# The second attention of a two-block layer: 64 units as one sequence, and the first branch's transposes beside projection panels

## What is computed

```python
def token_mixer(h, w_in, w_a2, b_a, b_f, g_gla, w_pa, w_pb, w_out):
    z = h @ w_in
    q_a, k_a, v_a, a_low, r_a, q_b, k_b, v_b, f_b, gate_a, gate_b = jnp.split(z, cuts, axis=-1)
    o_a = gla_chunked(heads(q_a * GLA_HK ** -0.5), heads(k_a), heads(v_a), heads(log_a))  # 4 heads
    o_a = rmsnorm_2(o_a, g_gla).reshape(B, T, GLA_DV) * jax.nn.silu(r_a)
    logf = jax.nn.log_sigmoid(f_b + b_f)
    o_b = fox_attention(heads(q_b), heads(k_b), heads(v_b), logf)       # 16 heads of 64
    merged = jax.nn.sigmoid(gate_a) * (o_a @ w_pa) + jax.nn.sigmoid(gate_b) * (o_b @ w_pb)
    return merged @ w_out
# fox_attention: logit[t,s] = q_t.k_s/8 + F_t - F_s with F = cumsum(logf), causal softmax, times v
```

## Time and profile before

| | |
|---|---|
| median of 3 runs | 2513.05 us (2510.02 to 2513.66) |
| the profiled execution | 2510.3 us, its span 2508.5 us |
| PE busy | 2365.5 us, 94% of the span |
| DVE, ACT, POOL busy | 948.3, 929.6, 1037.7 us |
| mean granted clock of PE | 0.961 of full speed |
| the stretch of the change | from 1703 to 1994 us of the span |

### The profile page before, as it was taken

How to read it: one execution, slowest core, us unless ns; L and a number is a source line. 1 busy time by engine, 2 the same in 40 slices (tenths; PEclk the granted TensorE clock), 3 DMA queues, 4 the chain that set the end, 5 groups by cost and what they waited for, 6 DMA issues and landing times.

```text
span 2508.5 us, 34111 instructions
## 1 busy us (share of the span) xinstructions
PE 2365.5 (94%) x10556; PEld 1922.4 (77%) x10556; DVE 948.3 (38%) x1601; ACT 929.6 (37%) x1628; POOL 1037.7 (41%) x796
## 2 busy tenths in 40 slices
PE   7999987899999998999997999998999997999997
PEld 6888866778888887888876777776666786888886
DVE  5699967435514214100114144444333343110012
ACT  4333374234322323333333533344333353443331
POOL 4455354444444443444453433332112254444443
PEclk9999998999999999999997999998899997999998
DMA  4334342437737432333331233333111331333331
GB/s 147 97 97 114 118 130 76 147 101 279 274 102 251 134 91 73 96 97 96 97 96 51 80 110 96 96 99 123 34 33 38 113 93 50 93 96 101 96 96 59
DMA packets 130557, 267.90 MB, mean 107 GB/s; under 512 B 14352, under 2 KB 14480, under 8 KB 129712
## 3 DMA queue, kind: packets, MB, share of 16 engines
q1 hardware_dynamic: 119520, 236.51, 31.4%
q10 hardware_dynamic: 10960, 30.38, 3.2%
HBM read 252.12 MB, written 14.68 MB: 106 GB/s over the span
## 4 chain that ended last, share of the span: by engine, by line
PE 82%; issue 7%; DVE 6%; POOL 3%; ACT 2%; DMA 0%; DVEq 0%; ACTq 0%; POOLq 0%
PE bank L851 24%; PE bank L853 23%; PE bank L852 23%; POOL wlo L374 2%; PE bank L1156 2%; PE bank L1188 1%; PE bank L1051 1%; PE bank L1053 1%; PE bank L1052 1%; PE bank L1102 1%; PE bank L1158 1%; PE bank L1170 1%; PE bank L1120 1%; DVE tmp L1507 1%; PE bank L961 1%
## 5 line engine op out<-in xcount | busy, mean ns | idle before, releaser
L374 POOL TENSOR_TENSOR wlo<-raw,whi 128x512 fp32r<-128x512 f32 x750 | 983.5, 1318 | 1365.9 <-ACT whi L446 1364.7
L851 PE MATMUL bank<-a_hi,whi 128*128 128x512 f32 x1992 | 797.0, 400 | 18.4 <-DVE a_lo L1261 7.1
L853 PE MATMUL bank<-a_lo,whi 128*128 128x512 f32 x1992 | 784.2, 394 | 0.0
L852 PE MATMUL bank<-a_hi,wlo 128*128 128x512 f32 x1992 | 784.0, 394 | 0.0
L446 ACT ACTIVATE whi<-raw 128x512 fp32r<-128x512 f32 x750 | 466.4, 627 | 776.6 <-PE bank L853 657.5
L851 PEld LDWEIGHTS bank<-a_hi,whi 128*128 128x128 f32 x1992 | 378.4, 190 | 113.6 <-issue 18.4
L853 PEld LDWEIGHTS bank<-a_lo,whi 128*128 128x128 f32 x1992 | 378.6, 190 | 80.8
L852 PEld LDWEIGHTS bank<-a_hi,wlo 128*128 128x128 f32 x1992 | 379.5, 191 | 74.5
L851 PE MATMUL bank<-b_hi,whi 128*128 128x512 f32 x788 | 316.5, 402 | 27.1 <-DVE G L1521 11.4
L852 PE MATMUL bank<-b_hi,wlo 128*128 128x512 f32 x788 | 312.1, 396 | 0.0
L853 PE MATMUL bank<-b_lo,whi 128*128 128x512 f32 x788 | 311.9, 396 | 0.0
(11 more groups left out here) (234 smaller groups left out, 1887.4 us busy)
## 6 DMA issues: line engine op xcount, KB each, us to landing
raw<-d_stream SPq DMA_DIRECT2D x750, 256.0 KB, 2.6
G<-d_ada SPq DMA_DIRECT2D x72, 512.0 KB, 4.6
spill_rv<-tmp ACTq DMA_DIRECT2D x32, 256.0 KB, 2.1
G<-spill_rv ACTq DMA_DIRECT2D x6, 1024.0 KB, 10.3
G<-d_x ACTq DMA_DIRECT2D x4, 512.0 KB, 5.4
spill_ga<-G ACTq DMA_DIRECT2D x8, 256.0 KB, 3.5
spill_gb<-G ACTq DMA_DIRECT2D x8, 256.0 KB, 3.5
G<-spill_ga ACTq DMA_DIRECT2D x1, 2048.0 KB, 8.1
```

Source lines behind the costliest of these rows:

```text
L374: pool.tensor_tensor(wlo[:, s % SRING, :], raw[:, s % RING, :], whi[:, s % SRING, :].bitcast(F32), ALU.subtract).then_inc(lo_done, 1)
L851: pe.matmul(out_ps, w_hi, hi[:, k, :], start=first and q == 0, stop=False)
L852: pe.matmul(out_ps, w_lo, hi[:, k, :], start=False, stop=False)
L853: mm = pe.matmul(out_ps, w_hi, lo[:, k, :], start=False, stop=last and q == len(ks) - 1)
```

## The change

Three things are done.

1. The four turns become one sequence of 64 units on PE, ACT and DVE, without loops: `scores(u + 2)` stands in every unit up to 61, and the first two scores stand once, ahead of everything. `QF`'s slots are chosen by the head's pair, and `keep_qk` follows in fixed units.
2. Tiles 2 and 3 of `qkb` are no longer done ahead. Two half panels follow the first two scores, and six stand between the eight groups of transposes of the first branch.
3. These transposes go to banks 4 and 5, since banks 6 and 7 now hold the scores of units 0 and 1. ACT takes their exponentials after the last product (`r_prod`) and ahead of its eight roundings, and DVE their maxima between the products and the scalings.

The work itself is the same: 64 half panels of `qkb` (16 ahead of unit 0's transposes, then one in each of 48 units), the same transposes, scores and products.

```diff
@@ -754,57 +755,61 @@
...
-def keep_qk(i, j):
+def keep_qk(j):
+    wait_used(act, "qkb", 0, 2 * j + 1)
     act.activation(QF[:, j % 4, :], bank_of("qkb", j)[:, :], ACT.Copy,
                    scale=FOX_HD ** -0.5 if j % 2 == 0 else 1.0).then_inc(evac_of("qkb", j), 1)
...
-for j in range(4):
+def fox_exp(u):
+    n = (u % 4 + 1) * P
+    act.wait_ge(fox_m, u + 1)
...
+for j in range(2):
     tick("qkb", 0, 2 * j)
-    wait_used(act, "qkb", 0, 2 * j + 1)
-    keep_qk(0, j)
-    if j == 1:
-        act.wait_ge(ld_r, 32)
-        for t in range(4):
-            act.activation(R2[:, t, :], R2[:, t, :], ACT.Silu).then_inc(r_silu, 1)
+    keep_qk(j)
+act.wait_ge(ld_r, 32)
+for t in range(4):
+    act.activation(R2[:, t, :], R2[:, t, :], ACT.Silu).then_inc(r_silu, 1)
+tick("qkb", 0, 4, 1)
+act.wait_ge(r_prod, 2 * GLA_HEADS)
+fox_exp(0)
+fox_exp(1)
 for m in range(KD):
     act.wait_ge(b_val, m + 1)
     act.activation(b_hi[:, m, :], tmp[:, m % 2, :], ACT.Copy).then_inc(b_hi_w, 1)
-def fox_turn(i, next_qk):
-    for u in range(17):
-        if u < 16:
-            n = (u % 4 + 1) * P
...
-        if next_qk and u < 16 and u % 2 == 0:
-            tick("qkb", i, 8 + u // 2, 1)
-        if not next_qk and u < 16 and u % 4 < 3:
-            tick("pa", 0, 3 * (u // 4) + u % 4, 1)
-        if next_qk and u in (9, 11):
-            keep_qk(i, 4 + u // 10)
-    if next_qk:
-        for j in (6, 7):
-            wait_used(act, "qkb", i, 2 * j + 1)
-            keep_qk(i, j)
-with act.Fori(0, FOX_HEADS // 4 - 1) as i:
-    fox_turn(i, True)
-fox_turn(FOX_HEADS // 4 - 1, False)
...
+    if m % 2 and m < 7:
+        tick("qkb", 0, 5 + m // 2, 1)
+    if m == 5:
+        keep_qk(2)
+for u in range(UNITS + 1):
+    if 2 <= u < UNITS:
+        fox_exp(u)
+    if u:
...
+        act.activation(PT[:, w % 2, 0:n], bank[4 + w % 2][:, 0:n], ACT.Copy).then_inc(fox_pt, 1)
+    if u == 1:
+        keep_qk(3)
+    if u < UNITS - 16:
+        if u % 2 == 0:
+            tick("qkb", 0, 8 + u // 2, 1)
+    elif u < UNITS and u % 4 < 3:
+        v = u - (UNITS - 16)
+        tick("pa", 0, 3 * (v // 4) + v % 4, 1)
+    if u > 8 and u % 8 in (1, 3) and u // 8 < 7:
+        keep_qk(2 * (u // 8 + 1) + u % 8 // 2)
...
@@ -1121,80 +1126,81 @@
...
-for j in range(4):
+def scores(u):
+    h, t = u // 4, u % 4
+    n = (t + 1) * P
+    r = slice(FOX_HD * (h % 2), FOX_HD * (h % 2 + 1))
+    at = h // 2 % 2 * 2
...
+def qk_half(q):
+    j, k = q // 4, 2 * (q % 4)
+    if k == 0:
+        bank_free("qkb", 0, j)
+    panel("qkb", 0, q // 2, (k, k + 1), bank_of("qkb", j)[:, :], OPA, k == 0, k == 6, q0=k % 4,
+          done=q % 2 == 1)
...
+for j in range(2):
     tile8("qkb", 0, j, OPA, opa, fill, False)
+pe.wait_ge(gla_exp, GLA_HEADS * len(GLA_EXP) + 1)
+scores(0)
+scores(1)
+qk_half(8)
+qk_half(9)
 pe.wait_ge(r_prod, 2 * GLA_HEADS)
 for m in range(KD):
     if m >= 2:
         pe.wait_ge(b_val, m - 1)
     for t in range(4):
-        mm = pe.transpose(bank[6 + m % 2][:, t * P:(t + 1) * P],
+        mm = pe.transpose(bank[4 + m % 2][:, t * P:(t + 1) * P],
                           ONH[:, m // 2, t, m % 2 * P:(m % 2 + 1) * P], ident)
     mm.then_inc(oa_t, 1)
+    if m < 6:
+        qk_half(10 + m)
...
-    scores(0)
-    scores(1)
-    for u in range(16):
-        h, t = u // 4, u % 4
-        pe.wait_ge(fox_p, i * 16 + (u + 3))
-        pe.wait_ge(fox_out, i * 16 + (u + 1))
-        for j in range(t + 1):
-            c = slice(j * P, (j + 1) * P)
-            mm = pe.transpose(bank[4 + u % 2][:, c], PR[:, u % 2, c], ident)
-        mm.then_inc(fox_t, 1)
-        if u < 14:
-            scores(u + 2)
-        if next_qk:
...
-with pe.Fori(0, FOX_HEADS // 4 - 1) as i:
-    fox_turn(i, True)
-fox_turn(FOX_HEADS // 4 - 1, False)
-pe.wait_ge(fox_out, 64 + 2)
+for u in range(UNITS):
+    h, t = u // 4, u % 4
+    pe.wait_ge(fox_p, u + 3)
+    if u < 2:
+        pe.wait_ge(b_val, KD - 1 + u)
+    pe.wait_ge(fox_out, u + 1)
+    for j in range(t + 1):
...
+    if u < UNITS - 2:
+        scores(u + 2)
+    if u < UNITS - 16:
+        qk_half(16 + u)
+    elif u % 4 < 3:
+        if u == UNITS - 16:
+            pe.wait_ge(opb, FILL_B["oa"] + KD)
+        pa_panel(3 * ((u - (UNITS - 16)) // 4) + u % 4)
+    pe.wait_ge(fox_pt, u + 3)
...
+dve.wait_ge(ld_f, 16)
+forget_sums(0)
...
+maximum(0)
+maximum(1)
...
-with dve.Fori(0, FOX_HEADS // 4 - 1) as i:
-    own.begin(i, 16 * 2)
-    fox_turn(i, False)
-    own.end(FOX_HEADS // 4 - 1)
-fox_turn(FOX_HEADS // 4 - 1, True)
+beside = [UNITS - 16 + u for u in (1, 4, 6, 9, 12, 14)]
+for u in range(UNITS):
+    h, t = u // 4, u % 4
+    if u < UNITS - 2:
+        maximum(u + 2)
+    if t == 0 and h < FOX_HEADS - 1:
+        forget_sums(h + 1)
```

More of the change, by code:

```diff
@@ L40 @@
 TAU = 16.0
+UNITS = 4 * FOX_HEADS
 RING, SRING, AHEAD = 8, 4, 3
@@ L1122, in _, with pa_panel @@
                         mm.then_inc(gla_mm, 1)
-            for j in range(4):
-                tile8("qkb", 0, j, OPA, opa, fill, False)
+            def scores(u):
[3 more added lines that the diff above has]
+                at = h // 2 % 2 * 2
+                s_ps = bank[6 + u % 2][:, 0:n]
+                pe.wait_ge(fox_p, u + 1)
+                if t == 0:
+                    pe.wait_ge(fox_nf, h + 1)
+                    wait_evac(pe, "qkb", 0, h // 2 * 2)
+                    wait_evac(pe, "qkb", 0, h // 2 * 2 + 1)
+                pe.matmul(s_ps, QF[r, at, t * P:(t + 1) * P], QF[r, at + 1, 0:n], start=True, stop=False)
+                pe.matmul(s_ps, ONES_R[32:64, :], NFH[32:64, h % 2, 0:n], start=False, stop=True)\
+                  .then_inc(fox_s, 1)
+            def qk_half(q):
[4 more added lines that the diff above has]
+                      done=q % 2 == 1)
+            def pa_panel(p):
+                if p % 2 == 0:
+                    bank_free("pa", 0, p // 2)
+                half = p % 2
+                panel("pa", 0, p, range(4 * half, 4 * half + 4), bank_of("pa", p // 2)[:, :], OPB, half == 0, half == 1)
+            for j in range(2):
+                tile8("qkb", 0, j, OPA, opa, fill, False)
+            pe.wait_ge(gla_exp, GLA_HEADS * len(GLA_EXP) + 1)
[3 more added lines that the diff above has]
+            qk_half(9)
             pe.wait_ge(r_prod, 2 * GLA_HEADS)
@@ L1193, in _ @@
-            with pe.Fori(0, FOX_HEADS // 4 - 1) as i:
-                fox_turn(i, True)
-            fox_turn(FOX_HEADS // 4 - 1, False)
-            pe.wait_ge(fox_out, 64 + 2)
+            for u in range(UNITS):
[5 more added lines that the diff above has]
+                for j in range(t + 1):
+                    c = slice(j * P, (j + 1) * P)
+                    mm = pe.transpose(bank[4 + u % 2][:, c], PR[:, u % 2, c], ident)
+                mm.then_inc(fox_t, 1)
+                if u < UNITS - 2:
[7 more added lines that the diff above has]
+                pe.wait_ge(fox_pt, u + 3)
+                for j in range(t + 1):
+                    mm = pe.matmul(bank[4 + u % 2][:, 0:FOX_HD], PT[:, u % 2, j * P:(j + 1) * P],
+                                   VB[:, j, h * FOX_HD:(h + 1) * FOX_HD], start=j == 0, stop=j == t)
+                mm.then_inc(fox_o, 1)
@@ L1198, in _ @@
+            pe.wait_ge(fox_out, UNITS + 2)
             for m in range(KD):
@@ L1790, in _ @@
-            with dve.Fori(0, FOX_HEADS // 4 - 1) as i:
-                own.begin(i, 16 * 2)
-                fox_turn(i, False)
-                own.end(FOX_HEADS // 4 - 1)
-            fox_turn(FOX_HEADS // 4 - 1, True)
+            beside = [UNITS - 16 + u for u in (1, 4, 6, 9, 12, 14)]
[5 more added lines that the diff above has]
+                    forget_sums(h + 1)
+                dve.wait_ge(fox_o, u + 3)
+                own.next(dve.reciprocal(small[:, 1, u % 2:u % 2 + 1], small[:, 5, t:t + 1]))
+                dve.tensor_scalar(OB[:, t, h * FOX_HD:(h + 1) * FOX_HD], bank[4 + u % 2][:, 0:FOX_HD],
+                                  small[:, 1, u % 2:u % 2 + 1], None, ALU.mult).then_inc(fox_out, 1)
+                if u in beside:
+                    keep_pa(beside.index(u))
```

107 lines of the change are left out of this document (25 added, 82 removed).

## The result

The changed kernel takes 2481.59 us, the median of 4 runs (2479.68 to 2487.65), beside 2513.36 for 4 runs of the kernel before (2510.02 to 2514.64). The ratio is 0.9884, with a 95% interval of 0.987 to 0.9898. The forecast was 2491 us with a range of 2486 to 2501, so the direction was right and the gain came out as 31.8 us instead of 21.6. Measured again beside other runs of the kernel before, the gain was 26.7 and 29.2 us (experiments 1 and 9), so some 3 to 5 us of the first figure are chance, and the rest of the miss is not.

A forecast was written before the change was run, and what follows sets the result against it. PE was taken to bound the kernel, gaining only where idle or at half clock. Seams 16.8, head 0 3.1 and unit 0's start 1.7 sum to 21.6 us, taking the median 2513.05 to 2491 us, range 2486 to 2501.

The forecast's parts named there:

- What bounds the kernel: Whole kernel: PE bounds it, so time is gained only where PE stands idle or runs at half clock.
- Behind unit 52, nothing: After unit 52: nothing changes; falls of the clock there may come or stay away, 1.7 us each.
- The seams, 16.8 us: Between the four turns: idle time and half clock at three seams, 7.53 + 6.35 + 2.92, all go, 16.8 us.
- Written-out code instead of a loop costs nothing: Attention turns: replacing the loop by written-out code has no cost, judged by turn 3, already written out.
- Pairs: Rival: scores of each new pair of heads wait for `keep_qk` at seven places, 2498 us and up; chance 0.04.
- Head 0, 3.1 us: Units 0 to 4: 3.37 us above a normal head, laid to half clock, mostly goes; gain 3.1 us.
- When unit 0 starts, 1.7 us: Start of the attention: unit 0's transposes begin at 1739.7 instead of 1741.44, a gain of 1.7 us.
- a pause of 3.8 us: Ahead of the first branch's transposes: PE newly waits for the products, from 1720.1 to 1723.9, 3.8 us.
- groups of 1.97 us: First branch's transposes: four transposes and a half panel take 1.97 us per group, six times, 11.8 us.
- The clock loss of 2.5 us: After the new pause: half clock delays unit 0 by 2.5 us, with ends of 0 and 8.5 us.
- Both together: Start of unit 0 and head 0: gains of 1.7 and 3.1 us, 4.8 us in all.
- The clock stays low at the start: Rival: half clock persists into head 0, costing 6.3 or 4.7 us, 2497 us in all; chance 0.22.

The follow-up runs named there:

- experiment 1: The changed kernel measured again with no edit: 2483.24 us, ratio 0.9894 to the kernel before.
- experiment 9: The changed kernel measured a third time with no edit: 2481.63 us, ratio 0.9879 to the kernel before.
- experiment 5: The kernel before the change, run once more with no edit for a second trace: 2508.03 us.
- experiment 10: The changed kernel plus 3 useless matmuls ahead of the wait for unit 0's scores and 16 ahead of the wait for the products: 2486.25 us.
- experiment 11: The changed kernel plus useless matmuls in the waits of the two double norms outside the change: 2487.33 us, ratio 0.9906.
- experiment 12: The changed kernel plus useless matmuls both at the new pause before unit 0 and in the two double norms: 2488.68 us, ratio 0.9911.
- experiment 2: The changed kernel, written out, but with no scores made across units 16, 32 and 48, so seams stay: 2494.90 us, ratio 0.9937.
- experiment 4: The kernel before with only its three looped turns written out on PE, ACT and DVE: 2504.42 us, ratio 0.9979.
- experiment 8: The changed kernel with the last 16 units' panels spread evenly, three blocks in every unit: 2484.08 us, ratio 0.9899.
- experiment 3: The kernel before with only the one sequence of 64 units, keeping the old start with four tiles ahead: 2492.95 us, ratio 0.9935.
- experiment 6: The one sequence with the old start, plus 33 useless matmuls where PE stood idle at that start: 2486.51 us, ratio 0.9908.

## Why the prediction was off, step by step

The traces can be added up stretch by stretch, which shows where the gain lies. The first pair is the two traces of the result, the second those of experiments 5 and 1:

| stretch (us) | before | after | gain | 5, before | 1, after | gain | predicted |
|---|---|---|---|---|---|---|---|
| up to the anchor | 1701.3 | 1697.5 | 3.8 | 1698.5 | 1701.0 | -2.5 | 0 |
| start and head 0 | 57.3 | 51.2 | 6.1 | 62.1 | 52.1 | 10.0 | 4.8 |
| units 4 to 60, with the seams | 217.3 | 200.4 | 16.9 | 213.0 | 200.5 | 12.6 | 16.8 |
| unit 60 to the end | 532.6 | 528.8 | 3.9 | 532.7 | 529.0 | 3.7 | 0 |
| span | 2508.5 | 2477.9 | 30.6 | 2506.2 | 2482.5 | 23.7 | 21.6 |

Start and seams together gave 22.9 and 22.6 us, 1.0 to 1.3 more than the 21.6 forecast. Ahead of the anchor nothing was changed, and the difference has either sign: that is chance. What lies behind unit 60 is the largest part of the miss that does not change sign.

- **What bounds the kernel.** Right. PE lost 21.1 us of busy time with the same matmuls, and where experiments 10 to 12 changed PE's clock or idle time at places where other engines decide, nothing was gained.
- **Behind unit 52, nothing.** This is the step that failed: "Behind unit 52 nothing changes; the falls of the clock there may come or stay away, 1.7 us each" left them out of the sum, and the stretch from unit 60 to the end became 3.9 and 3.7 us shorter. Both traces of the kernel before have two falls of 3.4 us there, first the result's, then experiment 5's:

```profile
1977.50:1980.90 3.40, 3.40 (x9) 2.63 (x9) 0.75 (x2) 0.00 (x0) 0.00 (x0) 0.50 0.27 77
1994.60:1998.00 3.40, 3.40 (x10) 2.63 (x10) 1.29 (x2) 1.44 (x3) 1.28 (x1) 0.51 0.88 376
```

```profile
1975.00:1978.40 3.40, 3.40 (x9) 2.72 (x9) 0.85 (x2) 0.00 (x0) 0.00 (x0) 0.51 0.22 77
1992.10:1995.50 3.40, 3.40 (x11) 2.72 (x10) 1.29 (x2) 1.60 (x3) 1.28 (x1) 0.50 0.84 347
```

  The first costs 1.6 us: from unit 60's transposes to the first transposes behind the last unit it is 1993.62 - 1975.87 = 17.75 us before and 1965.29 - 1949.13 = 16.16 after.

```profile
1975.87 0.28 PE L1170 MATMUL bank<-consts,G 128*128 128x128 f32 x1
1993.62 0.44 PE L1202 MATMUL bank<-consts,G 128*128 128x128 f32 x2 [0.58 <-DVE G L1784]
```

```profile
1949.13 0.28 PE L1187 MATMUL bank<-consts,G 128*128 128x128 f32 x1
1965.29 0.44 PE L1208 MATMUL bank<-consts,G 128*128 128x128 f32 x2 [0.58 <-DVE G L1789]
```

  The second costs another 1.6, and the double norm behind it takes 28.9 us in both traces of before, against 28.1 and 28.4. No trace without loops has both falls, and one of the twelve has the first (experiment 2). So they go with the loops, and most of the 5.5 us of experiment 4 may be they; why code that the change does not touch keeps its clock better stays open.
- **The seams, 16.8 us.** Right for the one trace it was read from, and 4.2 us too high for the other (12.6). In medians the seams alone are 11.5 to 11.7 us, and the idle time at the loops' ends 1.1 us more. The single seams are no constants: 7.53, 6.35 and 2.92 us in one trace and 6.4, 3.3 and 2.9 in another of the same kernel, by the length of the fall. "Written-out code instead of a loop costs nothing" compared heads in the middle of a turn and missed the loop's end, where PE is idle for 1.6 us instead of 1.13. Pairs did not become seams; no head in the middle took over 13.74 us in any trace of one sequence.
- **Head 0, 3.1 us.** This term was mis-sized, in the other direction. "The clock was half from 1731.7 to 1748.8 [...], so 7.36 us of it at half clock explain this" took the one fall of the earlier trace rows for the kernel's. Head 0 gained 2.6 us in the first pair and 7.4 in the second: two of four traces with the old start have a fall of 27.3 us, and head 0 takes 21.8 to 21.9 us in them.
- **When unit 0 starts, 1.7 us.** The steps were right: products ending 22.5 us behind the anchor (22.4 measured in experiment 9), a pause of 3.8 us (3.69 with the clock up), groups of 1.97 us (1.83). The clock loss of 2.5 us was somewhat too much: experiment 9, without a fall in this part, starts unit 0 at 35.36, and the traces with 3.4 to 6.8 us of half clock start it at 36.6 to 37.6, a loss of 1.3 to 2.2. The gain is 2.6 to 4.8 us, not 1.7.
- **Both together** were to give 4.8 us and gave 9.5 to 9.7 in the medians, without loops. In the traces it is 57.3 or 62 us against 51.2 to 52.1, or 55.5. The forecast was 52.4 after the change, so what comes after was nearly right. That the sum of start and seams came out so well is in part luck: the trace read had a short fall at the start and long ones at the seams, and against the second trace the two errors of 4 to 5 us cancel.
- **The rivals.** "The clock stays low at the start" was put at 0.22, and it happened in the traces of 8, 9, 10 and 12, two of them with useless matmuls ahead: head 0 took 5.6 us more, where 6 were written. In the others it did not. Traces of the changed kernel itself show both, so what was set against the forecast as another outcome is something that the same kernel does in some runs and not in others. Its runs lie between 2479.5 and 2487.9 us; whether this makes the difference between them can't be told from three traces.
- **What stays open.** Why the same code gets a fall of 17.1 us in one run and 27.3 in another. The falls hundreds of microseconds ahead of the change differ in the same way: the traces of 8, 9 and 10 have theirs at 361.2, 388.5 and 419.2 us within 0.1 us of each other and all fall for 13.7 us in unit 0, while the result's trace, with others from the start on, does not. Whether the one decides the other is not shown.

## What to carry to other kernels

Where an engine has a clock that falls behind thin work, don't price a single place by one trace, and don't stop at the places that are changed. Take two traces, cut the whole span into stretches and compare them all: here each of the two terms was off by 4 to 5 us against a second trace, their sum by 1, and 3.7 to 3.9 us lay in a stretch that was put at nothing. Put independent matmuls beside transposes and small products, since useful work in a thin stretch both fills it and keeps the clock (9.6 us here, of which useless matmuls in the same place got back 6.4). Before doing so, see who ends the waits there: at the norms, where POOL and DVE do, a higher clock bought nothing, and the added matmuls cost 5.7 us.

## What the runs showed that was not expected

- Useless matmuls can make a kernel faster: 33 of them, 6.4 us less (experiments 3 and 6). They can also raise the mean clock from 0.968 to 0.976 and make it slower by 5.7 us (9 and 11). The mean granted clock is no measure of the time.
- A pause of 3.69 us was followed by 15.2 us at full clock, in which PE was busy for 14.3, and only then the clock fell, for 13.7 us (experiment 9); in another run the clock fell within the same pause (1). Filling the pause moved the later fall by nothing (10).
- Once the heads follow each other without a seam, the clock holds for 255.5 us on end, with half a panel or a panel beside the small products of a unit and PE busy for 253.2 us of them; none of the nine traces of such kernels has a fall between head 1 and the last unit. Where seams are kept it fell behind each of the three, after 1.13 us of idle time with small matmuls around it (experiment 2).
